# In the expert stage, up is copied by ScalarE and multiplied by silu on GpSimd for six of seven slabs

## The reference: what is computed

```python
def swiglu(h, wg, wu, wd):
    return (jax.nn.silu(h @ wg) * (h @ wu)) @ wd
...
    logits = jnp.einsum('bsd,de->bse', h, router_w, preferred_element_type=jnp.float32)
    top_val, top_idx = lax.top_k(logits, TOP_K)
    gates = jax.nn.softmax(top_val, axis=-1)
...
        out = out + gate[..., e:e + 1] * swiglu(h, wg[e], wu[e], wd[e])
```

## Time and profile before

| | us |
|---|---|
| median of 3 runs (1378.38 to 1380.02) | 1379.0 |
| the profiled execution, its own time | 1380.6 |
| its span, first to last instruction | 1378.6 |
| TensorE busy in the span | 1359.6 (99%) |
| VectorE busy | 1193.6 (87%) |
| ScalarE busy | 1025.2 (74%) |
| GpSimd busy | 162.8 (12%) |
| transfers | 430.35 MB, 312 GB/s over the span |
| experts, first to last matmul | about 419 to 1370 |

### The profile page before, as it was taken

How to read it: one execution, slowest core, us unless ns; L and a number is a source line. 1 busy time by engine, 2 the same in 40 slices (tenths; PEclk the granted TensorE clock), 3 DMA queues, 4 the chain that set the end, 5 groups by cost and what they waited for, 6 DMA issues and landing times.

```text
span 1378.6 us, 20048 instructions
## 1 busy us (share of the span) xinstructions
PE 1359.6 (99%) x6885; PEld 1138.0 (83%) x6885; DVE 1193.6 (87%) x1450; ACT 1025.2 (74%) x1254; POOL 162.8 (12%) x128
## 2 busy tenths in 40 slices
PE   9999999999999999999999999999999999999998
PEld 7778999988988777888888788888878878887886
DVE  5876655568959989999999999999999999999999
ACT  5656444466758778888888888888888888888886
POOL 1020000000320242100400210040021003003000
PEclk9999999999999999999999999999999999999999
DMA  9944543633668999999999999999999999999980
GB/s 343 361 146 160 184 153 123 238 129 123 245 218 305 353 372 365 371 394 383 346 393 393 352 382 397 386 351 394 389 344 392 396 376 358 394 388 340 391 330 30
DMA packets 184479, 430.35 MB, mean 312 GB/s; under 512 B 6060, under 2 KB 14016, under 8 KB 184432
## 3 DMA queue, kind: packets, MB, share of 16 engines
q1 hardware_dynamic: 181136, 422.81, 82.8%
q0 software_dynamic: 3296, 6.92, 2.1%
HBM read 425.15 MB, written 7.36 MB: 314 GB/s over the span
## 4 chain that ended last, share of the span: by engine, by line
PE 88%; DVE 6%; ACT 2%; issue 2%; DMA 1%; POOL 0%; ACTq 0%; DVEq 0%; POOLq 0%
PE psum L777 28%; PE psum L779 28%; PE psum L778 27%; DVE w_lo L427 2%; PE psum L1347 2%; ACT xg_hi L1829 1%; DVE w_lo L409 1%; DMA slot_table<-routing,table_row 1%; DMA routing<-slot_table 1%; DVE xg_lo L2431 0%; PE psum L809 0%; PE psum L1208 0%; PE psum L910 0%; POOL slot_table L706 0%; DVE probs L2101 0%
## 5 line engine op out<-in xcount | busy, mean ns | idle before, releaser
L427 DVE TENSOR_TENSOR w_lo<-raw_ring,w_hi 128x1024 fp32r<-128x1024 f32 x674 | 810.0, 1222 | 43.7 <-ACT w_hi L422 1.4
L422 ACT ACTIVATE w_hi<-raw_ring 128x1024 fp32r<-128x1024 f32 x675 | 713.9, 1061 | 170.3 <-PE psum L779 169.6
L777 PE MATMUL psum<-w_hi,xg_hi 128*128 128x512 f32 x896 | 355.1, 396 | 4.3 <-DVE w_lo L427 4.2
L779 PE MATMUL psum<-w_hi,xg_lo 128*128 128x512 f32 x896 | 349.6, 390 | 0.0
L778 PE MATMUL psum<-w_lo,xg_hi 128*128 128x512 f32 x896 | 349.0, 390 | 0.0
L409 DVE TENSOR_TENSOR w_lo<-raw_ring,w_hi 128x1024 fp32r<-128x1024 f32 x124 | 151.5, 1228 | 77.7 <-ACT w_hi L401 76.8
L777 PEld LDWEIGHTS psum<-w_hi,xg_hi 128*128 128x128 f32 x896 | 168.3, 188 | 44.0 <-issue 10.5
L401 ACT ACTIVATE w_hi<-raw_ring 128x1024 fp32r<-128x1024 f32 x124 | 129.9, 1057 | 93.8 <-PE psum L779 93.6
L779 PEld LDWEIGHTS psum<-w_hi,xg_lo 128*128 128x128 f32 x896 | 168.2, 188 | 35.9
L778 PEld LDWEIGHTS psum<-w_lo,xg_hi 128*128 128x128 f32 x896 | 168.5, 188 | 33.1
L777 PE MATMUL psum<-w_hi,moe_hT_hi 128*128 128x512 f32 x448 | 175.9, 393 | 0.0
(11 more groups left out here) (297 smaller groups left out, 1440.1 us busy)
## 6 DMA issues: line engine op xcount, KB each, us to landing
raw_ring<-in_moe_w_gate SPq DMA_DIRECT2D x56, 2048.0 KB, 10.9
raw_ring<-in_moe_w_up SPq DMA_DIRECT2D x56, 2048.0 KB, 10.5
raw_ring<-in_moe_w_down SPq DMA_DIRECT2D x56, 2048.0 KB, 10.3
raw_ring<-in_ffn_w_gate SPq DMA_DIRECT2D x5, 2048.0 KB, 7.7
raw_ring<-in_ffn_w_up SPq DMA_DIRECT2D x5, 2048.0 KB, 15.5
raw_ring<-in_ffn_w_down SPq DMA_DIRECT2D x5, 2048.0 KB, 9.8
raw_ring<-in_w_in_ab SPq DMA_DIRECT2D x4, 2048.0 KB, 18.6
raw_ring<-in_w_in_cd SPq DMA_DIRECT2D x4, 2048.0 KB, 10.0
```

Of the source, the lines that this page charges most:

```text
L422: act.activation(wh[:, v % SPLITS, :], moe_raw(i, q), ACT.Copy).then_inc(hi_ready, 1)
L427: dve.tensor_tensor(wl[:, v % SPLITS, :], moe_raw(i, q), wh[:, v % SPLITS, :].bitcast(F32), ALU.subtract).then_inc(lo_ready, 1)
L777: pe.matmul(out_, sh, mh_, start=start, stop=False)
L779: return pe.matmul(out_, sl, mh_, start=False, stop=stop)
```

## The change

VectorE keeps `moe_h` only for slab 6. For slabs 0 to 5 ScalarE copies up from PSUM into `moe_h` behind the splits of step u, and GpSimd multiplies it there by `moe_silu`. To let GpSimd reach the products, they stand at chosen places between its other work. The gain moves from `xg_hi` and `xg_lo` to the quarter rows: GpSimd loads it to all partitions and multiplies where it copied, so that `gathered` works in two pieces per engine. ScalarE empties both halves of `moe_y`. `tables` moves from step d2 to g4, `turn_rows` from u5 to g6, and `pick_T` to GpSimd, behind its loop.

```diff
+            pool.dma_start(row_gain[:, :], norm_ffn[1].partition_broadcast(P)).then_inc(row_gain_loaded, 16)
+            pool.wait_ge(row_gain_loaded, 16)
             for t in range(TT):
                 pool.wait_ge(xs_rows_ready, t + 1)
-                pool.tensor_copy(xs_quarters[t][:, :, :].rearrange("p q (k i) -> p k q i", k=KD),
-                                 xs[:, t, :].rearrange("p (k q i) -> p k q i", k=KD, q=QUADS)).then_inc(xs_turned, 1)
+                pool.tensor_tensor(xs_quarters[t][:, :, :].rearrange("p q (k i) -> p k q i", k=KD),
+                                   xs[:, t, :].rearrange("p (k q i) -> p k q i", k=KD, q=QUADS),
+                                   row_gain[:, :].rearrange("p (k q i) -> p k q i", k=KD, q=QUADS), ALU.mult).then_inc(xs_turned, 1)
...
+            def first_gate_times_up(i):
+
+                pool.wait_ge(silu_ready, i + 1)
+                pool.wait_ge(up_ready, i + 1)
+                pool.tensor_tensor(mh[:, i % 2, :], msg[:, i % 2, :], mh[:, i % 2, :], ALU.mult).then_inc(h_ready, 1)
+
+            def gate_times_up(j, i):
+
+                gate = pool.snap(pool.to_reg(SLABS * j + (i + 1)))
+                pool.wait_ge(zeroed, 1)
+                pool.wait_ge(silu_ready, gate)
+                up = pool.snap(pool.to_reg((SLABS - 1) * j + (i + 1)))
+                pool.wait_ge(zeroed, 1)
+                pool.wait_ge(up_ready, up)
+                pool.tensor_tensor(mh[:, i % 2, :], msg[:, i % 2, :], mh[:, i % 2, :], ALU.mult).then_inc(h_ready, 1)
...
             def gathered(j):
...
-                for k in range(KD):
-                    if k % 4 == 0:
-                        act.wait_ge(xg_turned, 2 * j + (k // 4 + 1))
-                    g = gain_rows[3] + k
-                    ins = act.activation(xg_hi[:, k, :], xg_t[:, k, :], ACT.Copy, scale=colpar[:, g:g + 1])
-                    if k % 4 == 3:
-                        ins.then_inc(xg_hi_ready, 1)
+                for half in range(2):
+                    k4 = slice(4 * half, 4 * half + 4)
+                    act.wait_ge(xg_turned, 2 * j + (half + 1))
+                    act.activation(xg_hi[:, k4, :], xg_t[:, k4, :], ACT.Copy).then_inc(xg_hi_ready, 1)
...
-                act.activation(y[:, 0:512], bank(6), ACT.Copy, scale=rt[:, T_GSLOT:T_GSLOT + 1]).then_inc(y_act, 1)
+                act.activation(y[:, 0:512], bank(6), ACT.Copy, scale=rt[:, T_GSLOT:T_GSLOT + 1])
+                act.activation(y[:, 512:1024], bank(7), ACT.Copy, scale=rt[:, T_GSLOT:T_GSLOT + 1]).then_inc(y_act, 1)
...
+                    if kind == "u" and i < SLABS - 1:
+                        act.wait_ge(unit_used, j * JOB_UNITS + (U_MOE + 4 * v + 4))
+                        if i >= 2:
+                            act.wait_ge(hT_done, SLABS * j + (i - 1))
+                        act.activation(mh[:, i % 2, :], bank(2 + i % 2), ACT.Copy).then_inc(up_ready, 1)
...
-                        if kind == "u" and w == 4 * v + SPLITS + 3:
+                        if kind == "u" and i == SLABS - 1 and w == 4 * v + SPLITS + 3:
                             gate_times_up(j, v, i)
```

More of the change, by code:

```diff
@@ L734, in add_rows @@
                     compute_op=ALU.add).then_inc(rows_summed, 16)
+            def first_gate_times_up(i):
[10 more added lines that the diff above has]
+                pool.tensor_tensor(mh[:, i % 2, :], msg[:, i % 2, :], mh[:, i % 2, :], ALU.mult).then_inc(h_ready, 1)
             pool.wait_ge(sums_begun, 32)
             pool.memset(spare[:, 0:1], 0.0).then_inc(sums_free, 1)
+            first_gate_times_up(0)
+            first_gate_times_up(1)
             write_slots()
+            first_gate_times_up(2)
             load_slots()
+            first_gate_times_up(3)
             pool.wait_ge(tables_ready, 1)
@@ L745, in _ @@
             pool.wait_ge(slot_row_ready, 1)
+            first_gate_times_up(4)
             gather_rows()
+            first_gate_times_up(5)
             pool.wait_ge(meta_ready, 1)
@@ L753, in _ @@
                 pool.wait_ge(y_act, one)
-                pool.wait_ge(y_dve, one)
                 add_rows()
                 pool.tensor_copy(rt[:, T_GSLOT:T_GSLOT + 1], rt[:, bass.ds(j + T_SGATE, 1)]).then_inc(gate_row_ready, 1)
+                gate_times_up(j, 0)
                 added = pool.snap(pool.to_reg(16 * j))
@@ L770, in _ @@
                 gather_rows()
+                for i in range(1, SLABS - 1):
+                    gate_times_up(j, i)
+            pool.tensor_copy(rt[:, T_SROW:T_SROW + 1], rt[:, bass.ds(jobs + (T_STOK - 1), 1)]).then_inc(srow_ready, 1)
+            pool.wait_ge(srow_ready, 1)
+            for t in range(TT):
+                ins = pool.tensor_scalar(pick_t[:, t, :], cst[:, C_IOTA:C_IOTA + P], float(t * P),
+                                         rt[:, T_SROW:T_SROW + 1], ALU.add, ALU.is_equal)
+            ins.then_inc(pickT_ready, 1)
         @block.tensor
@@ L1866, in job @@
                         act.activation(msg[:, i % 2, :], bank(i % 2), ACT.Silu).then_inc(silu_ready, 1)
+                        if m is None and i == 1:
+                            act.wait_ge(xs_turned, TT)
                         if i >= 1:
                             turned_h(j, i - 1)
+                    if kind == "u" and i < SLABS - 1:
[3 more added lines that the diff above has]
+                        act.activation(mh[:, i % 2, :], bank(2 + i % 2), ACT.Copy).then_inc(up_ready, 1)
                     if kind == "d" and i == SLABS - 2:
@@ L2426, in gathered @@
             def gathered(j1):
-                for k in range(KD):
-                    if k % 4 == 0:
-                        dve.wait_ge(xg_hi_ready, 2 * j1 + (k // 4 + 1))
-                    g = gain_rows[3] + k
-                    ins = dve.scalar_tensor_tensor(
-                        out=xg_lo[:, k, :], in0=xg_t[:, k, :],
-                        scalar=colpar[:, g:g + 1], in1=xg_hi[:, k, :].bitcast(F32), op0=ALU.mult, op1=ALU.subtract)
-                    if k % 4 == 3:
-                        ins.then_inc(xg_lo_ready, 1)
+                for half in range(2):
+                    k4 = slice(4 * half, 4 * half + 4)
+                    dve.wait_ge(xg_hi_ready, 2 * j1 + (half + 1))
+                    dve.tensor_tensor(xg_lo[:, k4, :], xg_t[:, k4, :], xg_hi[:, k4, :].bitcast(F32),
+                                      ALU.subtract).then_inc(xg_lo_ready, 1)
             def first_gathered():
@@ L2539, in job @@
             def job(j, m):
-                if m is not None:
-                    y_out(m)
                 for w in range(AHEAD, SPLITS):
@@ L2557, in job @@
                         table_rows()
-                    if m is None and (kind, i) == ("d", 2):
+                    if m is None and (kind, i) == ("g", 4):
                         tables()
@@ L2563, in job @@
                         turned_h(j, i - 1)
-                    if kind == "u" and i == SLABS - 2:
+                    if kind == "g" and i == SLABS - 1:
                         turn_rows(j)
@@ L2573, in _ @@
                 job(m + 1, m)
-            for t in range(TT):
-                ins = dve.tensor_scalar(pick_t[:, t, :], cst[:, C_IOTA:C_IOTA + P], float(t * P),
-                                        rt[:, bass.ds(later + T_STOK, 1)], ALU.add, ALU.is_equal)
-            ins.then_inc(pickT_ready, 1)
             dve.wait_ge(xg_lo_ready, 2 * later + 4)
```

21 lines of the change are left out of this document (8 added, 13 removed).

## The result

| kernel | median us | runs | from, to |
|---|---|---|---|
| before, same chip | 1378.94 | 7 | 1377.85, 1380.02 |
| changed | 1384.35 | 7 | 1383.11, 1384.96 |

The changed kernel is slower: 1.0036 times the time of before, 95% interval 1.0026 to 1.0046. The forecast was 1376.1 with a range up to 1382.0; the measured time lies outside it.

A forecast was written before the change was run, and what follows sets the result against it. TensorE was taken to bound the kernel, busy 118.3 of 118.6 us in a job. Terms -4.9 + 0 + 1.2 + 3.7 - 1.6 - 1.3 = -2.9 us, from 1379.0, gave 1376.1; range 1372.3 to 1382.0.

The forecast's parts named there:

- seam: Between two jobs: shorter xg_hi and xg_lo let the first split end earlier, 0.7 us gained at each of seven, -4.9.
- product, steady slab: GpSimd's multiply of h in each slab: blocks VectorE, but TensorE does not wait for it, 0 per slab.
- (a): Job 0, before the first expert matmul: GpSimd multiplies the gain where it copied, which takes longer, +1.2 us.
- (b): Job 0: h of slab 2 stands behind the slot table's four stores on GpSimd, so TensorE's transposes wait, +3.7 us.
- (c): Job 0: tables move from d2 to g4, when their load has landed, so TensorE's wait goes, -1.6 us.
- tail: End of the kernel: pick_T made earlier on GpSimd and y_hi reached earlier through shorter xg_hi, -1.3 us.
- The port: VectorE and GpSimd exclude each other when both read SBUF; a product blocks VectorE, costed at 0 per slab.
- The 0.5 of the prediction: Steady slab: margin in us left before TensorE wants the split that GpSimd's product has blocked by about 1.1.
- Rival 1: Products hold the port for 2.0 us instead of 1.3, so 48 slabs lose 0.2 each: 1385.7, chance 0.14.

The follow-up runs named there:

- e3: The changed kernel with turn_rows in step d4 instead of g6; 1380.17 us.
- e2: The changed kernel with turn_rows back in step u5, where it was before the change; 1379.96 us.
- e5: e4 with GpSimd's second product of the gain waiting until VectorE has made the picks; 1373.08 us.
- e7: The kernel before with only the gain's part of the change, and the gain's second product waiting for the picks; 1371.64 us.
- e8: e5 with h of slab 2 in job 0 made by VectorE again; 1372.08 us.
- e10: e5 with one more GpSimd product per slab in slabs 1 to 5, into unused memory; 1382.48 us.
- e11: e5 with two more GpSimd products per slab in slabs 1 to 5, into unused memory; 1404.69 us.
- e4: The changed kernel with slab 2's product ahead of the slot table's stores in job 0 and turn_rows in step d4; 1375.59 us.
- e6: The kernel before with only the gain's part of the change (gain multiplied on GpSimd, xg_hi and xg_lo in two pieces); 1374.35 us.
- e12: e4 with the gain where it was before the change, xg_hi and xg_lo in eight pieces; 1378.09 us.
- e9: e7 with tables in step g4 and pick_T on GpSimd; 1371.55 us.
- e1: The changed kernel with slab 2's product ahead of the four stores of the slot table in job 0; 1380.17 us.

## Why the prediction was wrong

| term | forecast | in the traces |
|---|---|---|
| seam | -4.9 | -1.2, and +0.6 in the last job |
| product, steady slab | 0 | 0 |
| (a) gain's product | +1.2 | +1.3 |
| (b) h of slab 2 | +3.7 | +3.7 |
| clock behind (b) | not seen | +1.7 |
| (c) tables | -1.6 | -1.8 |
| tail | -1.3 | -1.1 |

- **The step that failed: the seam, -4.9.** What was said of xg_hi and xg_lo holds: with turn_rows elsewhere (e3) and the rest of the change as it is, jobs are 117.85 long, 0.73 less than before, against 0.7 forecast. What failed is the sentence under (c), "turn_rows moves a step later too". It stood there as harmless. By the prediction's own demands it should have been priced: two operations, 1.2 us of VectorE, past the moe_hT_lo of slab 5, into the only stretch of the job where VectorE has three operations beside its splits ahead of the seam. The margin there is below 1.2, and the wait came out as 0.6 in eight jobs. e2 and e3 show it: moved, 4.2 to 4.4 us come back. So the seam gave 1.2 where 4.9 was forecast, and the last job lost 0.6.
- **The second omission: the clock.** The 3.7 of (b) was right to 0.1, but not that the matmuls behind it run at half rate for 3.41 us. No row of before showed this: its longest wait in the experts, 1.60, was followed by matmuls at the usual distance. All executions of the three kernels with the late product (the changed one, e2, e3) have a mean clock of 0.997 or 0.998, but for one at 0.999; those of e5, e7 and e8 have 1.000. The mean alone is a weak sign: 24 of the 61 executions of before beside the experiments have 0.998 as well, with medians 0.2 to 0.7 us above those at 1.000, and why is not shown. The 1.7 rests on the trace of the changed kernel.
- **The port** was judged rightly in its result, with the block too large and the margin right. A product takes 0.8 us from VectorE, not 1.1. The 0.5 of the prediction is what is left behind a block of 1.1, so its whole margin is 1.6, and e10 and e11 give 1.5 and 1.8; the rival in e10's expectation took the 0.5 for the whole. The argument from the earlier trace rows, that GpSimd gets in only when VectorE pauses, doesn't hold for products: in e11 three of them alternate with the first three of six splits that stand back to back, each going ahead of the split that was issued after it. The Trainium skill (SBUF — State Buffer, Who interferes with whom) says that the one that issues first gets the port for its whole instruction; e11 agrees, and so does the copy of e7, 1.11 us long. The earlier trace rows does not fit it, and why that copy took 4.52 stays open.
- **Rival 1** (the port decides, 1385.7) came nearest to the measured time, and its cause was not the one: e4 has every product on GpSimd and is faster than before. A time near a rival's is no proof of the rival.
- **(a)** came as said, and e5 shows that it could have been avoided. **(c) and the tail** came out near their numbers, but not only for the reasons given. The 1.60 of (c) was read from one execution; with the tables unmoved the wait is none in e6 and 0.38 in e7. The tail's 1.1 is there in e7 without pick_T's move and is nearly gone in e12 with it, so it comes from the shorter xg_hi and xg_lo. In the medians tables and pick_T together give nothing that can be told (e9 against e7).

With the seam's and the clock's miss the sum becomes -2.9 + 4.3 + 1.7 = +3.1, near the +2.8 between the spans. The further 2.6 between the spans' difference and that of the medians is told above; part of it is that before's profile, on which the sum was built, was 1.6 above its median. The sum is thus one of two single executions: it takes (c) at the full size that the wait for the tables had in one of them.

## What to carry to other kernels

Price every moved operation at its new place as if it were added there, above all one that the change moves in passing: ask what is queued behind it and how much margin the last of these has. A relief of a busy engine is worth only what TensorE waited for it; here the products on GpSimd, the bulk of the change, were worth nothing (e12), and a smaller edit, the gain multiplied once ahead of the gather, was worth 7.3 us by itself (e7). Of the 7.3, seven seams give 5.2 and the tail 1.1. When a new wait of some microseconds is forecast on TensorE, add the time at half clock behind it: here 3.5 us of waiting cost 1.7 more. And a wait for a transfer, read from one execution, is not yet a term to be won: the one for the tables was 1.60, 0.38 and none in three traces.

## What was not expected of the hardware

- An idle time of 3.5 us of TensorE was followed by 3.41 us at half clock in each of the three profiles that have one, one of 2.06 in two of six profiles (e2, e3; not in the changed kernel, e1, e4, e6), those of 1.35 (e1) and 1.60 us (before) by none.
- GpSimd's product of 128x512 takes some 0.8 us away from a VectorE that splits without pause, though its own span reads 1.5 to 2.3 us: the span holds the wait for the split ahead of it.
- The load of the slot table reaches VectorE at different times behind GpSimd's last issue: 6.8 us in before, 5.8 in e7 and 4.8 in e6 (issues end at 480.81, 479.56 and 481.54, VectorE goes on at 487.61, 485.34 and 486.37).
